# Forget gates as steps of their own with two sets of buffers, one convolution product moved among the retention, and the first feed-forward gates at the row's step

## The reference, cut to what matters

```
# first block, per layer
xn = rmsnorm(h); hq, hf, hi, hgo, hz, nq, ... = split(xn @ w_in)
log_f = logaddexp(log(lb), log1p(-lb) + log_sigmoid(hf))     # forget gates, 4 heads of 128
k_hg  = (1 - lb) * sigmoid(-hf)
o_hg  = hgrn2_chunkwise(hq, log_f, k_hg, hi)                 # needs cumsum(log_f)
...  sparse attention, output product, gate with p[i]

# second block, per layer
a_x, a_c, a_b, q, k, v, g, z, gates = split(rmsnorm(x) @ w_in)
y_a = (a_b * conv3(a_c * a_x)) @ w_a_out                     # short convolution
y_b = (silu(g) * retention(rotary(q), rotary(k), v)) @ w_b_out
...  spatial gating, merge, cross-attention
x = x + (silu(h @ w1) * (h @ w3)) @ w2                       # feed-forward, h = rmsnorm(x)
```

## Time and profile before

| what | value |
|---|---|
| median of three runs | 3144.66 us |
| the profiled execution's own time | 3142.55 us |
| its span, first to last instruction | 3140.4 us |
| PE busy | 2849.6 us (91%), 13636 matmuls |
| DVE / ACT / POOL busy | 1232.0 / 1288.9 / 1150.4 us |
| mean granted TensorE clock | 0.949 |

### The profile page before, as it was taken

How to read it: one execution, slowest core, us unless ns; L and a number is a source line. 1 busy time by engine, 2 the same in 40 slices (tenths; PEclk the granted TensorE clock), 3 DMA queues, 4 the chain that set the end, 5 groups by cost and what they waited for, 6 DMA issues and landing times.

```text
span 3140.4 us, 40447 instructions
## 1 busy us (share of the span) xinstructions
PE 2849.6 (91%) x13636; PEld 2360.7 (75%) x13636; DVE 1232.0 (39%) x2186; ACT 1288.9 (41%) x2191; POOL 1150.4 (37%) x537
## 2 busy tenths in 40 slices
PE   8788789988888998899998999999889999899998
PEld 6677658767775787688786787877678787777887
DVE  4665672366567223343323331322433422232132
ACT  4443654454355352344443332423244443243242
POOL 3322343332234343144352344443224344234442
PEclk9899799999979999899999999999889999999999
DMA  4212102221210232133331233333122333123332
GB/s 130 71 42 58 48 1 88 79 74 29 68 54 1 72 107 73 34 102 100 95 121 47 81 94 96 93 94 105 54 67 88 101 103 99 54 87 95 94 94 94
DMA packets 270546, 242.32 MB, mean 77 GB/s; under 512 B 29376, under 2 KB 202624, under 8 KB 270336
## 3 DMA queue, kind: packets, MB, share of 16 engines
q1 hardware_dynamic: 267440, 235.12, 25.7%
q10 hardware_dynamic: 2896, 4.52, 0.4%
HBM read 237.51 MB, written 2.10 MB: 76 GB/s over the span
## 4 chain that ended last, share of the span: by engine, by line
issue 56%; POOL 29%; PE 12%; DVE 1%; POOLq 0%; ACT 0%; DVEq 0%; ACTq 0%
POOL wlo L2641 28%; PE bank L1776 2%; PE bank L1780 2%; PE bank L1779 2%; PE bank L1841 1%; PE bank L1845 1%; PE bank L1844 1%; POOL Ql L2633 0%; POOL dE L2633 0%; POOLq L2640 0%; POOL Kl L2633 0%; PE bank L1027 0%; POOL vv L2633 0%; PE bank L1000 0%; POOL At L2633 0%
## 5 line engine op out<-in xcount | busy, mean ns | idle before, releaser
L2641 POOL TENSOR_TENSOR wlo<-raw,whi 128x1024 fp32r<-128x1024 f32 (+2 forms) x440 | 1054.7, 2402 | 1802.7 <-ACT whi L1982 1802.3
L1982 ACT CAST whi<-raw 128x1024 fp32r<-128x1024 f32 (+2 forms) x443 | 456.5, 1034 | 737.7 <-PE bank L1841 504.6
L1776 PE MATMUL bank<-xhi,whi 128*128 128x512 f32 x928 | 369.7, 398 | 19.3 <-POOL wlo L2641 9.2
L1779 PE MATMUL bank<-xlo,whi 128*128 128x512 f32 x928 | 367.1, 396 | 0.0
L1780 PE MATMUL bank<-xhi,wlo 128*128 128x512 f32 x928 | 366.7, 395 | 0.0
L1841 PE MATMUL bank<-whi,xhi 128*128 128x512 f32 x832 | 332.8, 400 | 11.9 <-DVE xlo L2228 6.2
L1844 PE MATMUL bank<-wlo,xhi 128*128 128x512 f32 x832 | 329.3, 396 | 0.0
L1845 PE MATMUL bank<-whi,xlo 128*128 128x512 f32 x832 | 328.8, 395 | 0.0
L766 PE MATMUL bank<-whi,xhi 128*128 128x512 f32 (+2 forms) x704 | 266.3, 378 | 20.6 <-POOL wlo L2641 17.4
L769 PE MATMUL bank<-wlo,xhi 128*128 128x512 f32 (+2 forms) x704 | 260.1, 370 | 0.0
L770 PE MATMUL bank<-whi,xlo 128*128 128x512 f32 (+2 forms) x704 | 259.2, 368 | 0.0
(11 more groups left out here) (473 smaller groups left out, 5036.7 us busy)
## 6 DMA issues: line engine op xcount, KB each, us to landing
raw<-in_w_in SPq DMA_DIRECT2D x147, 512.0 KB, 3.7
raw<-in_w SPq DMA_DIRECT2D x132, 512.0 KB, 3.8
raw<-in_w_pg SPq DMA_DIRECT2D x16, 512.0 KB, 3.8
raw<-in_w_o SPq DMA_DIRECT2D x16, 512.0 KB, 3.8
raw<-in_xa_k SPq DMA_DIRECT2D x16, 512.0 KB, 3.9
raw<-in_xa_v SPq DMA_DIRECT2D x16, 512.0 KB, 3.8
raw<-in_xa_q SPq DMA_DIRECT2D x16, 512.0 KB, 3.8
raw<-in_xa_o SPq DMA_DIRECT2D x16, 512.0 KB, 3.8
```

Of the source, the lines that this page charges most:

```text
L1776: mm = pe.matmul(o, wh, rhs[0][:, k, :], start=(k == 0), stop=False)
L1779: pe.matmul(o, wh, rhs[1][:, k, :], start=False, stop=False)
L1982: nc.scalar.copy(whi[:, j % SLOTS, 0:nk * cols], raw[:, j % SLOTS, 0:nk * cols]).then_inc(hi_split, 1)
L2641: nc.gpsimd.tensor_tensor(wlo[:, s, 0:n], raw[:, s, 0:n], whi[:, s, 0:n].bitcast(F32), ALU.subtract).then_inc(lo_split, 1)
```

## The change

1. `forget_early` and `forget_late` become steps. `("fm", "hf", hh)` keeps only the scaling on DVE. The scaled input has four places (two in `dE`, two in `Kl`), the temporaries two sets (`tA`/`et 0`, `tB`/`sq 0`, `tC`/`sq 1`, `Ql 0`/`Ql 1`). A new semaphore, `forget_t`, tells that the sum of a head is made; ACT's second Exp/Ln pair of two heads before must be read by then. The new order is hf0 hf1 early0 hf2 early1 late0 hf3 early2 late1 v.0 early3 late2 v.1 late3 v.2.
2. In all norms but the cross-attention's, `turn_high` stands one `fm_low` earlier, with a `fm_low` behind it.
3. In the second block `ax 1` is no longer one of the first products: it is a whole product and stands first among those merged with the retention, so that each retention step now has other neighbours.
4. In the feed-forward the gates of `u 0`, `w 0` and `u 1` stand on ACT at `rows ffn`, behind three high parts.

```diff
     hq = fm("hq", "w_in", 0, HG)
-    s = [("fm_low", *x) for x in hq[:3]] + [("turn_high", "mix")] + hq[:3] + [("sums", "mix")] + hq[3:] + [("rows", "mix")]
-    s += fm("hf", "w_in", 512, HG) + merged_in(main, side, 4) + tm("kc", "w_in", 3072, 256, step=4)
+    low = [("fm_low", *x) for x in hq[:3]]
+    s = low[:2] + [("turn_high", "mix")] + low[2:] + hq[:3] + [("sums", "mix")] + hq[3:] + [("rows", "mix")]
+    hf = fm("hf", "w_in", 512, HG)
+    early, late = ([(f"forget_{x}", hh) for hh in range(HG)] for x in ("early", "late"))
+    s += hf[:2] + early[:1] + hf[2:3] + early[1:2] + late[:1] + hf[3:] + early[2:3] + late[1:2]
+    s += main[:1] + early[3:] + late[2:3] + main[1:2] + late[3:]
+    s += merged_in(main[2:], side, 2) + tm("kc", "w_in", 3072, 256, step=4)
...
-    first = fm("ax", "w_in_2", 0, 2) + conv[:1]
-    conv = conv[1:]
+    ax = fm("ax", "w_in_2", 0, 2)
+    first, conv = ax[:1] + conv[:1], ax[1:] + conv[1:]
...
-    s = [("fm_low", *x) for x in first] + [("turn_high", "mix")] + first + [("sums", "mix")] + g[:1] + [("rows", "mix")] + g[1:]
+    low = [("fm_low", *x) for x in first]
+    s = low[:1] + [("turn_high", "mix")] + low[1:] + first + [("sums", "mix")] + g[:1] + [("rows", "mix")] + g[1:]
...
-    s += [("fm_low", *x) for x in up[:3]] + [("turn_high", "ffn"), ("sums", "ffn")] + up[:3] + [("fm_low", *up[3]), ("rows", "ffn")]
+    low = [("fm_low", *x) for x in up[:3]]
+    s += low[:2] + [("turn_high", "ffn")] + low[2:] + [("sums", "ffn")] + up[:3] + [("fm_low", *up[3]), ("rows", "ffn")]
...
+        fx = (dE[:, 0, :], dE[:, 1, :], Kl[:, 0, :], Kl[:, 1, :])
+        fa, fb, fc, ft = (tA[:, :], et[:, 0, :]), (tB[:, :], sq[:, 0, :]), (tC[:, :], sq[:, 1, :]), (Ql[:, 0, :], Ql[:, 1, :])
...
-                link(nc.scalar.activation(tA[:, :], tA[:, :], ACT.Exp, scale=-1.0))
-                if hh:
-                    act.wait_ge(*b_ready.at(l, hh))
-                nc.scalar.activation(tB[:, :], tA[:, :], ACT.Ln, bias=1.0).then_inc(*fg_b.up())
+            def step_forget_early(step):
+                hh = step[1]
+                a, b = fa[hh % 2], fb[hh % 2]
+                act.wait_ge(*G.evacuated(("hf", hh), l))
+                link(nc.scalar.activation(a, fx[hh], ACT.Abs))
+                link(nc.scalar.activation(a, a, ACT.Exp, scale=-1.0))
+                if hh >= 2:
+                    act.wait_ge(*fg_t.at(l, hh - 1))
+                nc.scalar.activation(b, a, ACT.Ln, bias=1.0).then_inc(*fg_b.up())
...
+            def step_rows(step):
+                if step[1] == "ffn":
+                    gate(("u", 0), tA[:, :])
+                    gated(0)
+                    gate(("u", 1), tB[:, :])
```

More of the change, by code:

```diff
@@ L416, in steps_two @@
     return s[:-3] + [("turn_low", "mix")] + s[-3:]
-HALVED_TWO = [("ax", 0), ("ax", 1), ("ac", 0), ("u", 0), ("w", 0), ("u", 1), ("w", 1)]
+HALVED_TWO = [("ax", 0), ("ac", 0), ("u", 0), ("w", 0), ("u", 1), ("w", 1)]
 def groups_two(step):
@@ L717, in build @@
         rep_ready = signal("rep_ready")
-        fg_b, fg_c, fg_d, fg_k = (signal(f"forget_{c}")[0] for c in "bcdk")
+        fg_b, fg_c, fg_d, fg_k, fg_t = (signal(f"forget_{c}")[0] for c in "bcdkt")
         b_ready = signal("b_ready")[0]
@@ L1093, in square_place @@
                 n_sq[0] += 1
-                if i >= 2:
-                    act.wait_ge(*sigs["ss"].at(l, i - 1))
+                act.wait_ge(*(sigs["ss"].at(l, i - 1) if i >= 2 else fg_t.at(l, HG)))
                 return sq[:, i % 2, :]
@@ L1154, in step_fm, with step_forget_late @@
                     return
[L1155 to L1160 removed]
+            def step_forget_early(step):
[7 more added lines that the diff above has]
+                nc.scalar.activation(b, a, ACT.Ln, bias=1.0).then_inc(*fg_b.up())
+            def step_forget_late(step):
+                hh = step[1]
+                a, b = fa[hh % 2], fb[hh % 2]
                 act.wait_ge(*fg_k.at(l, hh + 1))
[L1162 removed]
+                nc.scalar.activation(kT[:, hh, :], fc[hh % 2], ACT.Exp, bias=lbc[:, 0, hh:hh + 1])
                 act.wait_ge(*fg_c.at(l, hh + 1))
[L1164 to L1165 removed]
+                link(nc.scalar.activation(b, a, ACT.Exp))
+                nc.scalar.activation(b, b, ACT.Ln, bias=1.0).then_inc(*fg_d.up())
             def step_tm(step):
@@ L1339, in scalar_one @@
             table = {"sums": step_sums, "z_gate": step_gate, "nz_gate": step_gate,
-                     "turn_low": step_turn_low, "turn_high": step_turn_high, "fm": step_fm, "tm": step_tm, "p_turn": step_p_turn, "hg_prep": step_hg_prep,
+                     "turn_low": step_turn_low, "turn_high": step_turn_high, "fm": step_fm,
+                     "forget_early": step_forget_early, "forget_late": step_forget_late, "tm": step_tm, "p_turn": step_p_turn, "hg_prep": step_hg_prep,
                      "hg_level": step_hg_level, "hg_out": step_hg_out, "hg_turn": step_hg_turn,
@@ L1408, in step_fm, with step_forget_early, step_forget_late @@
                     return
-                name, hh = step[1:3], step[2]
-                x, t = dE[:, hh % 2, :], Ql[:, 0, :]
-                c1, a, c1a = (lbc[:, i, hh:hh + 1] for i in range(3))
+                name = step[1:3]
                 dve.wait_ge(*G.filled(name, l))
-                tt_(x, G.ps(name)[:, :], row[:, :], ALU.mult).then_inc(*G.empty(name))
-                dve.wait_ge(*G.evacuated(name, l))
-                dve.wait_ge(*fg_b.at(l, hh + 1))
[L1416 to L1420, removed]
+                tt_(fx[step[2]], G.ps(name)[:, :], row[:, :], ALU.mult).then_inc(*G.empty(name))
+            def step_forget_early(step):
+                hh = step[1]
+                x, a, b, c, t = fx[hh], fa[hh % 2], fb[hh % 2], fc[hh % 2], ft[hh % 2]
+                c1, lowest, c1a = (lbc[:, i, hh:hh + 1] for i in range(3))
+                dve.wait_ge(*G.evacuated(("hf", hh), l))
+                dve.wait_ge(*fg_b.at(l, hh + 1))
+                link(stt(a, x, 0.0, b, ALU.min, ALU.subtract))
+                tt_(c, a, x, ALU.subtract).then_inc(*fg_k.up())
+                ts(t, a, c1, lowest, ALU.add, ALU.max)
+                link(ts(a, a, c1a, None, ALU.add))
+                stt(a, a, -1.0, a, ALU.mult, ALU.min).then_inc(*fg_c.up())
+            def step_forget_late(step):
+                hh = step[1]
+                t = ft[hh % 2]
                 dve.wait_ge(*fg_d.at(l, hh + 1))
-                link(tt_(t, t, tB[:, :], ALU.add))
+                tt_(t, t, fb[hh % 2], ALU.add).then_inc(*fg_t.up())
+                dve.wait_ge(*fg_t.at(l, hh + 1))
                 for c in range(TT):
@@ L1710, in vector_one @@
             table = {"sums": step_sums, "z_gate": step_z_gate, "nz_gate": step_nz_gate,
-                     "turn_low": step_turn_low, "turn_high": step_turn_high, "rows": step_rows, "fm": step_fm, "tm": step_tm, "p_turn": step_p_turn, "hg_prep": step_hg_prep,
+                     "turn_low": step_turn_low, "turn_high": step_turn_high, "rows": step_rows, "fm": step_fm,
+                     "forget_early": step_forget_early, "forget_late": step_forget_late, "tm": step_tm, "p_turn": step_p_turn, "hg_prep": step_hg_prep,
                      "hg_level": step_hg_level, "hg_kv": step_hg_kv, "hg_out": step_hg_out, "hg_turn": step_hg_turn,
@@ L2091, in step_fm, with gated @@
                     hi(kx8[:, 0, i, :], name, G.ps(name)[:, 0:MEM])
-                elif step[1] == "u":
-                    if i >= 2:
-                        act.wait_ge(*g_ready.at(l, i - 1))
+                elif name not in HALVED_TWO and step[1] == "u":
+                    act.wait_ge(*g_ready.at(l, i - 1))
                     gate(name, (tA, tB)[i % 2][:, :])
-                elif step[1] == "w":
-                    act.wait_ge(*G.evacuated(name, l))
-                    nc.scalar.copy(gT[:, 0, i % HALVES[0][1], :], et[:, (n_et[0] - 1) % 2, :]).then_inc(*hi_s.up())
+                elif step[1] == "w" and i:
+                    gated(i)
+            def gated(i):
+                act.wait_ge(*G.evacuated(("w", i), l))
+                nc.scalar.copy(gT[:, 0, i % HALVES[0][1], :], et[:, (n_et[0] - 1) % 2, :]).then_inc(*hi_s.up())
+            def step_rows(step):
[3 more added lines that the diff above has]
+                    gate(("u", 1), tB[:, :])
             def gelu():
@@ L2195, in step_xout @@
                     hi(xoT[:, 0, k] if k < 4 else xhi[:, k, :], ("xo", step[1], i))
-            table = {"sums": step_sums, "turn_low": step_turn_low, "turn_high": step_turn_high, "mem": step_mem, "fm": step_fm, "tm": step_tm,
+            table = {"sums": step_sums, "turn_low": step_turn_low, "turn_high": step_turn_high, "rows": step_rows, "mem": step_mem, "fm": step_fm, "tm": step_tm,
                      "ret_pair": step_ret_pair, "ret_out": step_ret_out, "ret_turn": step_ret_turn, "sg_w": step_sg_w, "sg_norm": step_sg_norm,
@@ L2256, in step_rows @@
                 if step[1] == "mix":
-                    for i in range(2):
```

(10 more changed lines are left out.)

## The result

The changed kernel takes 3053.1 us in the median (3049.9 to 3059.0, four runs), the kernel before 3144.5 us (3143.5 to 3147.6, four runs): 91.4 us less, ratio 0.971 with the interval 0.9698 to 0.9722. The sign was right and the waits went where they were expected to go, but the gain was 26 us larger. The profiled execution took 3055.2 us, its span is 3053.2 us, so the span fell by 87.2 us.

A forecast was written before the change was run, and what follows sets the result against it. PE was taken as the bound, other engines mattering where they let it wait. Forget gates 21.7, turns 11.1, retention 20 and feed-forward gates 12.4 sum to 65.2 us less than 3144.7: 3079 us, range 3066 to 3092 (3059 to 3104 with rivals).

The forecast's parts named there:

- The step that failed: Retention: waits fall from 18.4 to 13.1 us and 10 of 15 us low clock goes; 20 us in both layers.
- Turns: At six norms, PE's waits of 2.2 to 2.3 us behind the high half's turn go: 11.1 us, bounds 8 and 13.7.
- the new one of 2.5 us: Ahead of the turn in layer 0 of the second block, PE waits 2.6 us for the last residual sum.
- Forget gates: Forget-gated heads: PE's waits for POOL's low parts and the low clock go, 21.7 us in both layers.
- the new wait: At `hg_prep`, PE arrives at 94.1 us and DVE is ready at 96.1 us: 2.1 us of wait per layer.
- The price of a split: At the forget gates, each POOL split costs DVE about 2.1 us; eight cost up to 17 us.
- the upper bound of 25.9: At the forget gates, the gain in both layers is 25.9 us if DVE is in time.
- Feed-forward gates: At the third `u`, the 4.58 us wait and 1.6 us of low clock go: 12.4 us in both layers.
- 1: At the forget gates, DVE becomes the bound and the part gives 6 us: 3095 us in all; chance 0.14.
- 4: In the retention, the lower clock holds and 30 us a layer is lost: 3160 us, 15 us slower; chance 0.03.
- 2: The retention gains nothing: its waits move and the clock stays as it is, 3100 us; chance 0.15.
- Rival 3: All four parts: all covers hold and the clock stays up in the retention, 84 us less, 3061 us; chance 0.12.

The follow-up runs named there:

- r1_order: The changed kernel with the retention's steps in another order, the two convolution products with long VectorE work no longer adjacent: 3020.8 us, ratio to before 0.9612.
- filled forget gates: The kernel before with unread identity matmuls in three waits of each layer, at the forget gates and the feed-forward: 3143.1 us, ratio 0.9992.
- r3_filled: `r1_order` with unread identity matmuls ahead of nine kinds of steps whose wait is 2.3 to 5.8 us: 2996.7 us, ratio to before 0.9539.

## Why the prediction was wrong in size

**The step that failed** is in the retention: "The low clock costs 15 us now ...; with fewer and shorter waits I take two thirds of it, 10 us. That is 5.3 + 5 = 10 us a layer". The stock of 15 us was nearly right. Before, the stretch from the row's step to `mg_turn` takes 341.8 us, with the product ax 1 added (5.46) 347.3 us; `r1_order`, with 1.0 us of the retention's waits left, takes 313.7 us. Of the 33.6 us between them 17.4 are idle time and 16.2 clock (in layer 1 35.2 us, 16.9 and 18.3). These are the windows in layer 0, of before, of the changed kernel and of `r1_order`:

```profile
1160.41:1502.17 341.76, 318.16 (x1394) 260.39 (x1392) 133.21 (x190) 132.70 (x189) 123.25 (x51) 0.94 0.26 77
1125.91:1456.99 331.08, 314.76 (x1418) 257.96 (x1416) 130.77 (x190) 133.76 (x190) 127.17 (x52) 0.96 0.28 82
1129.90:1443.58 313.68, 307.36 (x1418) 252.61 (x1416) 130.11 (x190) 133.48 (x190) 126.26 (x52) 0.99 0.29 86
```

The share that goes was wrong. The changed kernel takes 331.1 us there in layer 0 and 328.6 us in layer 1, 16.2 and 18.7 us less than 347.3. The retention's idle time fell from 18.4 to 11.1 us and from 17.9 to 10.4, so 7.3 and 7.5 us are idle time and 8.9 and 11.2 are clock, where I had 5.3 and 5. So some 7 us of low clock were left in each layer, not 10. I had taken the clock nearly in proportion to the idle. The records show the lower level for 37.6 us of layer 0's retention before, in four stretches, each over or behind one of the four waits over 2 us (2.40, 4.80, 4.81 and 5.28 us), and for 20.5 us after, in two, one of them around the only such wait left, the 6.36 us. This term was 14.8 us of the 26 missing; the turns and the forget gates were 4.3 us each.

**Turns: the same omission, smaller.** The old waits went, and the new one of 2.5 us in layer 0 of the second block came as worked out. No clock was priced, and it had fallen behind the turn in layer 1 of both blocks (0.92 and 0.91 in the windows of before from 584.6 and 2140.9 us, about 1.7 us of time each); it is 1.00 there now. That is most of what makes 15.4 us out of 11.1. Behind waits of the same length in layer 0 of both blocks the clock had stayed at 1.00, so part of this term is chance.

**Forget gates: the loss was right, the new wait was not.** 14.1 and 11.8 us were lost before, and to 0.1 us all of it is back. The price of a split for DVE was right, as DVE's timeline of the kernel after shows:

```profile
56.50 2.63 DVE L1438 TENSOR_SCALAR Ql<-tA,lbc 128x512 f32<-128x512 f32 x1
63.07 2.77 DVE L1440 SCALAR_TENSOR_TENSOR et<-et 128x512 f32<-128x512 f32 x1
81.20 1.37 DVE L1450 TENSOR_TENSOR_SCAN bT<-ones,Ql 128x128 f32<-128x128 f32 x4
83.19 5.61 DVE L1450 TENSOR_TENSOR_SCAN bT<-ones,Ql 128x128 f32<-128x128 f32 x4
```

with POOL's splits beside them (the last line two of them):

```profile
55.91 2.94 POOL L2679 TENSOR_TENSOR wlo<-raw,whi 128x1024 fp32r<-128x1024 f32 x1 [3.05 <-ACT whi L2008]
62.60 2.68 POOL L2679 TENSOR_TENSOR wlo<-raw,whi 128x1024 fp32r<-128x1024 f32 x1 [3.75 <-ACT whi L2008]
82.91 4.98 POOL L2679 TENSOR_TENSOR wlo<-raw,whi 128x1024 fp32r<-128x1024 f32 x2 [2.90 <-ACT whi L2008]
```

Each split holds one instruction of DVE for about 2.1 us: four scans take 1.37 us without and 5.61 us beside two splits, 2 x 2.1 more. But I charged all eight, and the first (50.5 us) fell into DVE's own waiting. DVE was done with what `hg_prep` needs at 92.9 us, which is 94.5 us on the time axis of before (the row's step is 1.6 us earlier in this trace), not at 96.1. PE came when it was expected (94.2 us on that axis, worked out as 94.1) and waited 0.4 us instead of 2.1. The 26 us are the upper bound of 25.9 that the prediction gave.

**Feed-forward gates: right in their mechanism**, 12.7 us of 12.4; that the sum fits so well is luck, since the layers gave 4.7 and 8.0 us instead of 6.2 each. The wait of 4.58 us and the low clock behind it are gone in both. The rest is low clock behind the waits of 2.3 us further on, which this part does not touch: one stretch in each layer before, two in layer 0 and none in layer 1 after. Of the rivals, 1 and 4 needed a backlog or a clock that did not come, 2 would have left the retention as it was. Rival 3, all covers hold, was the nearest with 3061 us. It priced the retention at 32 us with the clock staying up; 34.8 us came with 11 us of waits left and the clock at 0.88.

## What to carry to other kernels

Where PE is the bound, price a wait as its own length plus the clock that follows it, and take back both when it goes: in this retention 18 us of waits a layer carried 16 to 18 us of clock with them. But count the clock only where PE's pace moves the next step; between two waits for a chain on other engines it was free, as layer 1 of the filled forget gates showed. And spread products that bring another engine work between those that bring none, before looking for less work.

## What the runs showed of the hardware that was not expected

Useless matmuls in a wait make a kernel faster: 12.4 and 8.2 us in the two layers of the old retention, 24 us in `r3_filled`. In the trace of `r1_order` 36 of the 43 stretches at the lower level begin within 2.7 us of the end of a wait of 1.7 us or more, and they last 3.4 to 13.7 us. It did not always help: behind `v 3` in layer 0 of the filled forget gates, 2.4 us of filler followed by 3.25 us of idle, the clock fell all the same; in layer 1, after the same filler and 3.23 us of idle, it stayed up. Which part of a wait has to be filled was not tried.
